# Ends of two expert stages: last down matrix in halves, output gates applied ahead of the 0/1 product, next first tile by column halves

## The chip, the cores and the metric

The kernel runs on one core of one Trainium2 chip. The metric is the device time of one execution in microseconds (us), the median of several runs. All data are 32-bit floats. A profiled execution comes with it, whose times below count from the start of its span. PE is the matrix engine (PEld its weight loads), DVE the vector engine, ACT the scalar engine, POOL the third elementwise engine; SP issues DMAs.

## What is computed

The program is a two-layer transformer block with mixture-of-experts layers, followed by a second, dense block of one layer. What matters here is the end of each expert layer, the residual sum, and the normalisation and projection that come next. D is 1024, a layer has 32 experts with an inner width of 512, and each token goes to two of them.

```python
f = _hier_moe(tokens, ...)        # per expert: (silu(x @ w_gate[e]) * (x @ w_up[e])) @ w_down[e]
                                  # out[token] += weight * result, for two experts per token
x = x + g2 * f[:b * s]            # g2: the output gates, one value per column
...
h = _modulate(_rmsnorm(x, norm1_g[i]), sh1, sc1)   # layer 1 starts: norm, then times (1+scale), plus shift
q, k, v = _project(h, w_qkv, splits)
...
return _rmsnorm(x, final_g)       # end of the first block
...
h = rms_norm(x, attn_norm_g) @ w_in                # second block starts
```

## The kernel before, in words

Each layer's expert stage is `experts` (L2200 to L2674). Tokens are grouped in blocks of 64 for one expert. For block i, PE multiplies the turned tokens by the gate matrix and the up matrix (`expand`, L2401), ACT and DVE form the hidden values, PE turns them (L2438), and `contract` multiplies them by the down matrix (L2447): 16 matmul records of 512 columns. The result `down` lies in PSUM with the two column halves of D on the two halves of the partitions, 64 tokens each. DVE copies it to `y` (L2632) and POOL scatters its rows into the DRAM tensor `y_dram` (`moe_results` in the trace). A ring of three slots holds each expert's three 2 MB matrices; SP issues the loads (`load_gate`, `load_up`, `load_down`) when a slot has been read, all in one queue.

Block 31, the last, is treated apart. Its rows are not waited for from DRAM. PE makes its `down`; ACT copies that to `ring["y"]` (L2521); PE multiplies a matrix of zeros and ones, `hit`, by that copy (`last_part`, L2127), which puts the rows of the head tile (the first tile of 128 tokens that the next stage takes up) in token order in the PSUM tiles `gate[0]` and `up[0]`, one for each half of the columns. DVE meanwhile adds up the other experts' share of that tile. The order on DVE is written out by hand, each instruction waiting for the one before:

- multiply the gates by the tile's weight of its last expert, `share` (L2663), once the gates are in;
- wait for `ys`, both result rows of each token of the head tile (`ys_in`), scale and add them (L2665, L2666), multiply by the gates (L2668), add to the residual `res` (L2669);
- wait for the 0/1 product (`part_done`), and for each column half multiply it by the scaled gates (L2673) and add it to `res` (L2674).

SP's order is: the gates broadcast to 128 partitions, 512 KB (L2299); wait until the scatters of the blocks before have landed; `ys`, 1 MB (L2302); then the next stage's first weights and vectors (`enter_1_loads`, `enter_2_loads`). The gates and `ys` lie in the ring's third down slot (`moe_wd` in the trace). A barrier of all engines ends the stage, and the next stage begins on the other side of it.

After layer 0 that is `enter_layer_1`: POOL scatters the last block's rows (L2135), SP then reads the results of the next tile and its gates (L2787, L2788). DVE norms the head tile (L2867, L2869), PE turns its eight column groups (L2923), ACT copies them to SBUF in two halves (L2811), and PE starts the projections (L2949), three chunks of eight matmuls. Before the third chunk PE turns the first chunk's rotated heads (L2932). For these it waits on DVE, whose order is norm of the head tile, sum of the next tile (`combine`, L2850 to L2853, behind its gates and results), rotation of the first chunk (L192 to L203).

After layer 1 it is `enter_block_2`: DVE applies both norms in one pass (L3244), PE turns (L3348), ACT copies (L3159), and PE does five chunks (L3362). In both stages PE runs some transposes of the identity (L1582) while it waits for the norm.

## Time and profile before

| what | value |
|---|---|
| median of 3 runs | 2636.52 us (2635.07 to 2636.66) |
| the profiled execution's own time | 2634.72 us |
| its span | 2632.8 us |
| PE busy | 2351.5 us (89%) |
| DVE busy | 1242.7 us (47%) |
| ACT busy | 571.0 us (22%) |
| layer 0's expert stage | about 590 to 1079 us of the span |
| layer 1's expert stage | about 1410 to 1888 us |

The times of the page are averages over stages with different limits. The part of the program that the change touches is short: some 20 us at the end of each expert stage and the beginning of the next. It is read from the timeline there, which lists instructions in order of time, with the idle time of the engine in brackets and what ended it.

### The profile page before, as it was taken

To read this page: it belongs to the slowest core of one execution; us is meant where nothing else is said; L and a number is where in the kernel's file an instruction comes from. 1 tells how busy PE (TensorE), PEld (TensorE's weight loads), DVE (VectorE), ACT (ScalarE), POOL (GpSimd) and SP (SyncE) were. 2 spreads that over 40 slices of the span, in tenths; PEclk is the share of its full clock that TensorE was granted. 3 is DMA by queue.
4 is the path that set the end of the run, shared out by engine and by line. 5 is a ranking of instruction groups with operands and counts; after the bars stand their busy time and mean duration, and the time that the engine had idled before them with its cause. 6 is when DMAs were issued, how large, how long until landed. Compare 5 with 4: busy or idle time off the path is not lost. (4 is left out here: it accounts for less than half of the span.)

```text
span 2632.8 us, 32518 instructions
## 1 busy us (share of the span) xinstructions
PE 2351.5 (89%) x12743; PEld 1383.2 (53%) x12743; DVE 1242.7 (47%) x2503; ACT 571.0 (22%) x1347; POOL 169.1 (6%) x268
## 2 busy tenths in 40 slices
PE   7999898988987777798998998788799899999999
PEld 4455666555543333445656553343344665888444
DVE  3367788754322222475655322222355653445665
ACT  4000487210100000115541100000122552111000
POOL 0000000002211111000001111111000000000000
PEclk9999999999999999999999999999999999999999
DMA  8774500449999999714019999999820221232643
GB/s 304 263 276 150 230 12 1 180 171 396 423 425 426 425 425 427 280 68 147 1 66 391 424 423 426 425 425 425 354 90 0 77 75 46 65 96 76 212 160 128
DMA packets 133380, 619.45 MB, mean 235 GB/s; under 512 B 21248, under 2 KB 48296, under 8 KB 103528
## 3 DMA queue, kind: packets, MB, share of 16 engines
q1 hardware_dynamic: 122664, 596.30, 57.1%
q0 software_dynamic: 10560, 21.01, 2.1%
q8 instruction: 105, 1.72, 0.3%
q14 instruction: 51, 0.42, 0.0%
HBM read 600.40 MB, written 30.47 MB: 240 GB/s over the span
## 5 line engine op out<-in xcount | busy, mean ns | idle before, releaser
L2401 PE MATMUL moe_gate<-moe_wg,moe_xg_t 128*64 128x256 f32 x1984 | 241.1, 394 | 49.1 <-DMA moe_wg<-in_moe_w_gate 47.5
L2401 PE MATMUL moe_up<-moe_wu,moe_xg_t 128*64 128x256 f32 x1984 | 239.2, 392 | 42.2 <-DMA moe_wu<-in_moe_w_up 42.2
L2447 PE MATMUL moe_down<-moe_wd,moe_hid_t 128*64 128x512 f32 x1024 | 235.5, 601 | 43.9 <-DMA moe_wd<-in_moe_w_down 30.8
L2401 PEld LDWEIGHTS moe_gate<-moe_wg,moe_xg_t 128*64 128x64 f32 x1984 | 147.5, 136 | 159.9 <-DMA moe_wg<-in_moe_w_gate 81.4
L2401 PEld LDWEIGHTS moe_up<-moe_wu,moe_xg_t 128*64 128x64 f32 x1984 | 146.1, 135 | 130.8 <-DMA moe_wu<-in_moe_w_up 60.6
L3847 PE MATMUL mlp_acc<-m_h,mlp_w 128*128 128x256 f32 x896 | 196.3, 382 | 5.3 <-DVE c_buffer L4024 2.5
L2632 DVE COPY moe_y<-moe_down 128x512 f32<-128x512 f32 x62 | 42.9, 692 | 308.1 <-PE moe_down L2447 308.1
L3847 PEld LDWEIGHTS mlp_acc<-m_h,mlp_w 128*128 128x128 f32 x896 | 171.0, 191 | 30.4 <-issue 4.1
L2447 PEld LDWEIGHTS moe_down<-moe_wd,moe_hid_t 128*64 128x64 f32 x1024 | 74.0, 137 | 161.2 <-issue 124.0
L2495 ACT ACTIVATE moe_sig<-moe_gate 128x256 f32<-128x256 f32 x64 | 24.5, 383 | 540.0 <-PE moe_gate L2401 540.0
L2619 DVE TENSOR_SCALAR moe_sig<-moe_sig 128x256 f32<-128x256 f32 x62 | 18.3, 294 | 257.3 <-ACT moe_sig L2495 257.3
L2621 DVE RECIPROCAL moe_sig<-moe_sig 128x256 f32<-128x256 f32 x62 | 108.7, 1753 | 2.1
L2336 POOL DMA_INDIRECT moe_results<-moe_y,moe_y_idx x62 | 64.2, 1035 | 705.3 <-DVE moe_y L2632 705.3
L2488 ACT COPY moe_xg_t<-moe_x_tp 128x512 f32<-128x512 f32 x64 | 37.4, 585 | 303.7 <-PE moe_x_tp L2385 303.7
L3898 PE MATMUL mlp_acc<-mlp_w,mlp_s_t 128*128 128x512 f32 x176 | 79.1, 592 | 0.0
L1117 ACT ACTIVATE dif_prob<-dif_score,dif_neg_max 128x768 f32<-128x768 f32 (+1 forms) x96 | 73.3, 764 | 13.9 <-DVE dif_neg_max L1049 9.7
L973 PE MATMUL dif_score<-a_k,a_q 64*128 64x256 f32 (+1 forms) x320 | 62.9, 504 | 14.8 <-ACT dif_prob L1117 12.5
L1333 DVE CUSTOM_DVE_ANT_0 swa_masked<-swa_score,b_masks,b_sinks 128x512 f32<-128x512 f32 (+1 forms) x64 | 52.1, 815 | 45.9 <-issue 32.3
L2627 DVE TENSOR_TENSOR moe_hid<-moe_sig,moe_up 128x256 f32<-128x256 f32 x62 | 26.1, 421 | 96.6 <-PE moe_up L2401 96.5
L2102 POOL DMA_INDIRECT moe_xg<-moe_tokens,moe_x_idx x62 | 64.6, 1042 | 49.0 <-POOL moe_x_idx L2312 48.2
L3898 PE MATMUL mlp_acc<-mlp_w,mlp_u_t 128*128 128x512 f32 x132 | 61.2, 592 | 0.0
L1006 PE MATMUL dif_out<-a_v,dif_prob_t 128*128 128x128 f32 x448 | 59.1, 278 | 2.2 <-ACTq L1134 0.9
(599 smaller groups left out, 3704.2 us busy)
## 6 DMA issues: line engine op xcount, KB each, us to landing
moe_wg<-in_moe_w_gate SPq DMA_DIRECT2D x64, 2048.0 KB, 41.9
moe_wu<-in_moe_w_up SPq DMA_DIRECT2D x64, 2048.0 KB, 42.8
moe_wd<-in_moe_w_down SPq DMA_DIRECT2D x64, 2048.0 KB, 42.4
qkv_mod_w<-in_mod_w SPq DMA_DIRECT2D x42, 1024.0 KB, 6.2
mlp_w<-in_w_down SPq DMA_DIRECT2D x44, 512.0 KB, 5.7
mlp_w<-in_w_up SPq DMA_DIRECT2D x16, 1024.0 KB, 8.0
qkv_w<-in_a_w_qkv SPq DMA_DIRECT2D x12, 1024.0 KB, 10.5
m_h<-in_w_down SPq DMA_DIRECT2D x20, 512.0 KB, 6.1
```

The source lines that it names most:

```text
L973: mm = nc.tensor.matmul(unit(g, m)[:, n0:n0 + w], q_t[rows, h, t * P:(t + 1) * P], k_t[rows, h, n0:n0 + w], start=True, stop=True)
L1006: mm = nc.tensor.matmul(out[:, 0:P], prob_t[:, g % 2, k, :], v[:, k, h * P:(h + 1) * P], start=(k == 0), stop=(k == keys(g) - 1))
L1117: nc.scalar.activation(prob[:, g % 3, m, 0:width], unit(g, m)[:, 0:width], ACT.Exp, bias=neg_max[:, g % 2, m:m + 1], accum_out=total[:, g ...
L1333: nc.vector.tensor_tensor_reduce(masked[:, g % 2, m, 0:width], score[m][:, 0:width], masks[:, b, 0:width], 1.0, sinks[:, 2 * c + m:2 * c + ...
L2102: nc.gpsimd.indirect_dma_start(ring["xg"][b][:], None, token_halves, bass.IndirectOffsetOnAxis(ap=places, axis=0), bounds_check=last_token ...
L2336: nc.gpsimd.indirect_dma_start(result_halves, bass.IndirectOffsetOnAxis(ap=y_idx[b][:], axis=0), y[b][:], None, bounds_check=last_result, ...
L2401: mm = nc.tensor.matmul(acc[b][halves[f], 0:HF], x_t[:, k, c, :], w[:, c, k, :].rearrange("p (q f j) -> p f q j", f=2, j=2)[:, f], start=( ...
L2447: mm = nc.tensor.matmul(down[b][halves[c], :], hid_t[:, k, h, :], wd[z][:, 2 * h + k, c * NCHUNK:(c + 1) * NCHUNK], start=(k, h) == (0, 0) ...
L2621: nc.vector.reciprocal(sig[:], sig[:]).then_inc(s["step"], 1)
L2632: nc.vector.tensor_copy(y[b][:], down[b][:]).then_inc(s["y_done"], 1)
L3847: mm = nc.tensor.matmul(acc[z][:, 0:half], lhs[:, k, j * P:(j + 1) * P], right_up(b)[:, k, :], start=(x < 4 and k == 0), stop=(k == 3), sk ...
L3898: mm = nc.tensor.matmul(bank(q, x)[:], lhs, rhs[:, f, :], start=(i == 0), stop=(i == 2 * MLP_GROUPS - 1), skip_group_check=True)
```

## The change

The last expert's down matrix comes in two DMAs, one for each half of the hidden values, each with a semaphore of its own; `contract` goes through the hidden values half by half (for all blocks, with the same matmuls), and for the last block waits for the second half in the middle. SP also loads the gates a second time as 64 rows by 512 columns for each column half, to the partitions where `down` holds that half. DVE no longer scales the gates by `share`. After it has added the other experts' share it multiplies `down` by those gates into `gated_y`; PE's 0/1 product reads `gated_y`; and DVE adds the product times `share` to `res`, one instruction for each column half. ACT's copy of `down` to `ring["y"]`, now only needed for the scatter, waits for `gated_y`. In the next stage, the head tile's norm is done by column halves, and PE's turns and first products wait for halves.

```diff
@@ load_down_in_halves, new
+    rows = e["moe_w_down"][layer].rearrange("x (p h k) n -> x p h (k n)", h=2, k=2)
+    for half, landed in enumerate((ring["d_in"][b], ring["tail_in"])):
+        part = ring["wd"][b][:, 2 * half:2 * half + 2, :]
+        sp.dma_start(part.rearrange("p a n -> p (a n)"), rows[x][:, half]).then_inc(landed, 16)
@@ experts, sync
+                if isinstance(x, int) and x == last:
+                    load_down_in_halves(sp, e, layer, ring, b, x)
+                else:
+                    load_down(sp, e, layer, ring, b, x)
...
             sp.dma_start(gates, bcast_rows(mod_part(e, layer, 5)(0))).then_inc(s["gates_in"], 16)
+            for half in range(2):
+                columns = mod_part(e, layer, 5)(0)[half * NCHUNK:(half + 1) * NCHUNK]
+                sp.dma_start(gates_by_half[HALVES[half], :], columns.partition_broadcast(HD)).then_inc(
+                    s["gates_in"], 16)
             sp.wait_ge(s["landed"], 2)
@@ contract
-                for k in range(2):
-                    for h in range(2):
+                for h in range(2):
+                    if h and by_halves:
+                        pe.wait_ge(ring["tail_in"], 16)
+                    for k in range(2):
@@ tensor, last block
-            pe.wait_ge(s["y_l_done"], 1)
-            last_part(nc, ring, part).then_inc(s["part_done"], 1)
+            pe.wait_ge(s["gated_done"], 1)
+            last_part(nc, ring, gated_y, part).then_inc(s["part_done"], 1)
@@ scalar, last block
-            act.wait_ge(s["downed"], i + 1)
+            act.wait_ge(s["gated_done"], 1)
             nc.scalar.copy(ring["y"][:], down[last % 2][:]).then_inc(s["y_l_done"], 1)
@@ vector, last block
-            link(v.tensor_scalar(gated_share, gates, ring["share"][:], None, ALU.mult))
...
             link(v.tensor_tensor(res, res, ys[:, 0, :], ALU.add))
+            dve.wait_ge(s["downed"], i + 1)
+            v.tensor_tensor(gated_y, down[b][:], gates_by_half, ALU.mult).then_inc(s["gated_done"], 1)
             dve.wait_ge(s["part_done"], 1)
             for half in range(2):
                 cols = slice(half * NCHUNK, (half + 1) * NCHUNK)
-                link(v.tensor_tensor(ys[:, 0, cols], part[half], gated_share[:, cols], ALU.mult))
-                link(v.tensor_tensor(res[:, cols], res[:, cols], ys[:, 0, cols], ALU.add))
+                link(v.scalar_tensor_tensor(res[:, cols], part[half], ring["share"][:], res[:, cols], ALU.mult,
+                                            ALU.add))
@@ enter_layer_1, vector (tile 0 by halves; enter_block_2 has the like in first_norms)
-                link(v.scalar_tensor_tensor(h[:], e["res"][:, t, :], rstd[:, one],
-                                            mul[:, side(t), :], ALU.mult, ALU.mult))
-                v.tensor_tensor(h[:], h[:], add[:, side(t), :], ALU.add).then_inc(s["h_done"], 1)
+                width = D if i else NCHUNK
+                for n0 in range(0, D, width):
+                    cols = slice(n0, n0 + width)
+                    link(v.scalar_tensor_tensor(h[:, cols], e["res"][:, t, cols], rstd[:, one],
+                                                mul[:, x, cols], ALU.mult, ALU.mult))
+                    v.tensor_tensor(h[:, cols], h[:, cols], add[:, x, cols], ALU.add).then_inc(s["h_done"], 1)
@@ both, tensor
-                pe.wait_ge(s["h_done"], i + 1)
                 for half in range(2):
+                    pe.wait_ge(s["h_done"], i + 2 if i else 1 + half)
...
+                    if j == 0 and k % 4 == 0:
+                        pe.wait_ge(s["n_tp_read"], 1 + k // 4)
```

On DVE, at the end of layer 0's expert stage (layer 1's reads the same), stood before, from the last hidden values on (`moe_wd` is the slot that holds the gates and `ys`, `moe_gate` and `moe_up` hold the 0/1 product's halves):

```order
L2659 TENSOR_TENSOR moe_hid<-moe_sig,moe_up 128x256
L2663 TENSOR_SCALAR moe_wd<-moe_wd,moe_last_share 128x1024
L2665 TENSOR_SCALAR moe_wd<-moe_wd,r_weight 128x1024
L2666 SCALAR_TENSOR_TENSOR moe_wd<-moe_wd,r_weight 128x1024
L2668 TENSOR_TENSOR moe_wd<-moe_wd 128x1024
L2669 TENSOR_TENSOR res<-res,moe_wd 128x1024
L2673 TENSOR_TENSOR moe_wd<-moe_gate,moe_wd 128x512
L2674 TENSOR_TENSOR res<-res,moe_wd 128x512
L2673 TENSOR_TENSOR moe_wd<-moe_up,moe_wd 128x512
L2674 TENSOR_TENSOR res<-res,moe_wd 128x512
```

The sums over the other experts' results (the rows from L2665 to L2669) stand between the scaled gates and the use of the product.

On DVE, at the same place, stands now (`moe_wd` on the left of `moe_down` is `gated_y`):

```order
L2678 TENSOR_TENSOR moe_hid<-moe_sig,moe_up 128x256
L2683 TENSOR_SCALAR moe_wd<-moe_wd,r_weight 128x1024
L2684 SCALAR_TENSOR_TENSOR moe_wd<-moe_wd,r_weight 128x1024
L2686 TENSOR_TENSOR moe_wd<-moe_wd 128x1024
L2687 TENSOR_TENSOR res<-res,moe_wd 128x1024
L2689 TENSOR_TENSOR moe_wd<-moe_down,moe_wd 128x512
L2693 SCALAR_TENSOR_TENSOR res<-moe_gate,moe_last_share,res 128x512
L2693 SCALAR_TENSOR_TENSOR res<-moe_up,moe_last_share,res 128x512
```

The pass over 1024 columns ahead of the sums is gone; behind them one pass of 512 from `down` is new, and the four of 512 behind the product have become two.

On SP, in the same stage, from the gates on, stood before:

```order
L2299 DMA moe_wd<-mod_scratch 128x1024
L2302 DMA moe_wd<-moe_results 128x2x1024
L2178 DMA moe_wu<-in_norm_g 128x1024
L2181 DMA moe_wg<-mod_scratch 128x1024
L2182 DMA moe_wg<-mod_scratch 128x1024
L2172 DMA moe_wg<-in_b_w_qkv 128x8x512
```

The second row is `ys`, the results of the head tile; the rows after it are the next stage's.

On SP, at the same place, stands now:

```order
L2312 DMA moe_wd<-mod_scratch 128x1024
L2315 DMA moe_wd<-mod_scratch 64x512 x2
L2319 DMA moe_wd<-moe_results 128x2x1024
L2187 DMA moe_wu<-in_norm_g 128x1024
L2190 DMA moe_wg<-mod_scratch 128x1024
L2191 DMA moe_wg<-mod_scratch 128x1024
L2181 DMA moe_wg<-in_b_w_qkv 128x8x512
```

Two broadcasts of 64 by 512 have come between the gates and `ys`.

On DVE, at the entry of layer 1, from the end of the head tile's inverse root on, stood before:

```order
L167 TENSOR_TENSOR qkv_rstd<-qkv_rstd,qkv_tmp 128x1
L2867 SCALAR_TENSOR_TENSOR qkv_h<-res,qkv_rstd,moe_wg 128x1024
L2869 TENSOR_TENSOR qkv_h<-qkv_h,moe_wg 128x1024
L2850 TENSOR_SCALAR qkv_ys<-qkv_ys,r_weight 128x1024
L2851 SCALAR_TENSOR_TENSOR qkv_ys<-qkv_ys,r_weight 128x1024
```

The norm of the tile is the second and third row; the sum of the next tile follows.

On DVE, at the same place, stands now:

```order
L167 TENSOR_TENSOR qkv_rstd<-qkv_rstd,qkv_tmp 128x1
L2890 SCALAR_TENSOR_TENSOR qkv_h<-res,qkv_rstd,moe_wg 128x512
L2892 TENSOR_TENSOR qkv_h<-qkv_h,moe_wg 128x512
L2890 SCALAR_TENSOR_TENSOR qkv_h<-res,qkv_rstd,moe_wg 128x512
L2892 TENSOR_TENSOR qkv_h<-qkv_h,moe_wg 128x512
L2870 TENSOR_SCALAR qkv_ys<-qkv_ys,r_weight 128x1024
L2871 SCALAR_TENSOR_TENSOR qkv_ys<-qkv_ys,r_weight 128x1024
```

The two passes over the tile have become four over its column halves.

## Rows read from the trace of the kernel before

**Rows 1.** Timeline, end of layer 0's expert stage: start us, us, engine, line, operation [idle before]

```profile
1055.34 0.33 SPq L2299 DMA_DIRECT2D moe_wd<-mod_scratch  x1
...
1066.09 0.37 SPq L2302 DMA_DIRECT2D moe_wd<-moe_results  x1
...
1070.86 0.58 ACT L2521 COPY moe_last_y<-moe_down 128x512 f32<-128x512 f32 x1 [3.93 <-PE moe_down L2447]
...
1071.59 0.66 PE L2127 MATMUL moe_gate<-moe_last_y,moe_last_hit 64*128 64x512 f32 x1 [0.77 <-ACT moe_last_y L2521]
...
1071.65 0.75 DVE L2665 TENSOR_SCALAR moe_wd<-moe_wd,r_weight 128x1024 f32<-128x1024 f32 x1 [2.82 <-DMA moe_wd<-moe_results]
...
1072.13 0.59 PE L2127 MATMUL moe_up<-moe_last_y,moe_last_hit 64*128 64x512 f32 x1
...
1075.02 1.22 DVE L2669 TENSOR_TENSOR res<-res,moe_wd 128x1024 f32<-128x1024 f32 x1
...
1076.28 0.69 DVE L2673 TENSOR_TENSOR moe_wd<-moe_gate,moe_wd 128x512 f32<-128x512 f32 x1
...
1078.45 0.69 DVE L2674 TENSOR_TENSOR res<-res,moe_wd 128x512 f32<-128x512 f32 x1
```

**Rows 2.** Timeline, end of layer 1's expert stage

```profile
1876.67 3.65 PE L2447 MATMUL moe_down<-moe_wd,moe_hid_t 128*64 128x512 f32 x16 [0.75 <-DMA moe_wd<-in_moe_w_down]
...
1880.74 0.75 DVE L2665 TENSOR_SCALAR moe_wd<-moe_wd,r_weight 128x1024 f32<-128x1024 f32 x1 [2.16 <-DMA moe_wd<-moe_results]
```

**Rows 3.** DMA issues (KB each, median us to landing): end of layer 0's stage

```profile
moe_wd<-moe_results SPq DMA_DIRECT2D x1, 1024.0 KB, 5.5
...
moe_wd<-mod_scratch SPq DMA_DIRECT2D x1, 512.0 KB, 12.7
```

**Rows 4.** DMA issues: end of layer 1's stage, then three loads into an idle queue

```profile
moe_wd<-moe_results SPq DMA_DIRECT2D x1, 1024.0 KB, 5.1
...
qkv_ys<-moe_results SPq DMA_DIRECT2D x3, 1024.0 KB, 5.2
```

**Rows 5.** Windows of 1 us: busy of the engines, granted clock, DMA share, GB/s

```profile
1077.00:1078.00 1.00, 0.00 (x0) 0.00 (x0) 0.96 (x2) 0.00 (x0) 0.00 (x0) 0.50 1.02 379
...
1886.00:1887.00 1.00, 0.00 (x0) 0.00 (x0) 0.93 (x3) 0.00 (x0) 0.00 (x0) 0.50 0.00 0
```

**Rows 6.** One line's instructions: duration ns min/median/max (the product of 512 columns)

```profile
L2949 PE MATMUL qkv_acc<-moe_wd,b_buffer x96: 592/592/1222, 1102.9 to 1201.6; 128*128 128x512 f32 x96
```

**Rows 7.** Timeline, entry of layer 1's projections

```profile
1080.68 1.13 POOL L2135 DMA_INDIRECT moe_results<-moe_last_y,moe_last_y_idx  x1 [22.61 <-issue]
...
1082.22 1.28 DVE L2867 SCALAR_TENSOR_TENSOR qkv_h<-res,qkv_rstd,moe_wg 128x1024 f32<-128x1024 f32 x1
...
1086.73 7.10 PE L2949 MATMUL qkv_acc<-moe_wg,b_buffer 128*128 128x512 f32 x16 [0.82 <-ACT b_buffer L2811]
...
1095.56 0.75 DVE L2850 TENSOR_SCALAR qkv_ys<-qkv_ys,r_weight 128x1024 f32<-128x1024 f32 x1 [10.79 <-DMA moe_wu<-mod_scratch]
...
1102.45 0.66 PE L2932 MATMUL qkv_tp<-ident_sb,qkv_stage 128*128 128x128 f32 x4 [1.75 <-DVE qkv_stage L203]
```

**Rows 8.** DMA over layer 1's entry (1072 to 1095 us): total, two issues

```profile
DMA packets 4469, 8.89 MB, mean 387 GB/s; under 512 B 1215, under 2 KB 1215, under 8 KB 4466
...
moe_wu<-in_b_w_qkv SPq DMA_DIRECT2D x1, 2048.0 KB, 10.9
...
qkv_rope<-const_axial SPq DMA_DIRECT2D x1, 256.0 KB, 11.6
```

**Rows 9.** Timeline, entry of the second block

```profile
1893.38 1.28 DVE L3244 SCALAR_TENSOR_TENSOR c_buffer<-c_buffer,in_n_rstd,res 128x1024 f32<-128x1024 f32 x1
...
1894.73 1.73 PE L3348 MATMUL in_tp<-ident_sb,c_buffer 128*128 128x128 f32 x8 [0.41 <-DVE c_buffer L3244]
...
1897.22 7.11 PE L3362 MATMUL in_acc<-moe_wg,in_h_tile 128*128 128x512 f32 x16 [0.77 <-ACT in_h_tile L3159]
```

**Rows 10.** Windows: the second block's projections from their first product

```profile
1897.00:2035.00 138.00, 135.60 (x350) 63.74 (x351) 69.41 (x174) 32.10 (x68) 0.00 (x0) 1.00 0.21 77
```

33 lines of the change are left out of this document (20 added, 13 removed).

## Prediction

> **What bounds the kernel now.** I read the page's first parts only to see that no single engine bounds the program, then the timeline at the ends of the two expert stages, where everything that is changed lies, then the DMA issues, the granted clock, and the entries of the two stages behind. For each wait on the way to the end of a stage the question is what came last.
>
> At the end of layer 0's expert stage there are two branches [rows 1]. PE's branch ends early: the 0/1 product starts at 1071.59 and is done at 1072.13 + 0.59 = 1072.72 us. DVE's branch is late: it waits for `ys` until 1071.65, sums until 1075.02 + 1.22 = 1076.24, and turns to the product at 1076.28, when that has lain ready for 3.6 us. The last addition ends at 1078.45 + 0.69 = 1079.14, and nothing else is at work. So the path is: landing of `ys`, four passes on DVE (4.6 us), and a tail of 1079.14 - 1076.24 = 2.90 us. The down matrix and the copy on ACT are not on it. Layer 1 reads alike: `ys` ends the wait at 1880.74, while the last down product began at 1876.67 and runs 3.65 us, to 1880.32 [rows 2].
>
> **The change, part by part.** *The down matrix in halves.* In layer 1 PE waited 0.75 us at most in front of the last down product [rows 2]; whatever of it goes, goes from the branch that is early by 3.6 us. I take 0. The second DMA issue costs SP some 0.4 us (the issues of rows 1 take 0.33 and 0.37) while it has nothing to do before 1066.09. The other order of hidden halves leaves every block's matmuls as they were: 0.
>
> *The gates once more.* Their 2 x 128 KB stand ahead of `ys` in SP's queue. At the 387 GB/s of a full queue [rows 8] 0.26 MB take 0.7 us. Is the queue still at work when `ys` comes? In layer 0 the gates were issued at 1055.34 and took 12.7 us, to 1068.04 [rows 1, 3], 2 us after `ys` was issued at 1066.09; `ys` took 5.5 us [rows 3], where the same megabyte takes 5.2 us in an idle queue [rows 4]. So it was held up a little, and I take 0.6 us. In layer 1 `ys` took 5.1 us [rows 4] and was not held up; most of the 0.7 falls into the gap, and I take 0.2. The bounds are 0 and 0.7 in each.
>
> By the ring order of one queue on each DMA engine (the Trainium skill, "DMA: Bandwidth & Descriptors", section "Queues, rings and completion order": descriptors are consumed in ring order) the two broadcasts would hold back `ys` by their whole 0.7 us in layer 1 too, and the sum below would be 0.5 us more; the 5.1 us beside 5.2 speaks for a queue that had run dry by then, and no run here shows the new broadcasts.
>
> *DVE's removed pass.* The scaled gates (1024 columns, 0.75 us like L2665) lay in the wait for `ys`: 0.
>
> *The tail.* This is the main term. Before: four passes, 2.90 us. Now, counted from the same 1076.24: `gated_y`, a two-operand pass from PSUM of 512 columns like L2673, 0.04 + 0.69; the hand-over to PE, as from ACT's copy (ends 1071.44) to the product (1071.59), 0.15; the product; the hand-over back, 0.06; two passes with a scalar of 512 columns. Their price is 0.75 each: over 1024 columns such a pass takes 1.28 [rows 7] and one without the scalar 1.22 [rows 1], so the scalar adds 0.06 to L2673's 0.69. With 0.04 between them they make 1.54. The product took 1.13 us at full clock [rows 1]. But PE has by then been idle since the last down product, in layer 0 from 1070.82 (ACT's copy follows at 1070.86) to about 1077.7, and the granted clock after the product of before had fallen to 0.50 by 1077 and by 1886 [rows 5], the lower level of 1.2 GHz, with PE idle since 1072.72 and about 1882. One 512-column matmul record runs 592 ns at full clock and up to 1222 when slowed [rows 6]; twice 1.13 is 2.3, less what is not the array's, and I take 2.2. The tail is 0.73 + 0.15 + 2.2 + 0.06 + 1.54 = 4.68 us, **1.78 longer** in each stage; at full clock it is 3.61, 0.71 longer. The product, which lay beside DVE's sums, now lies behind them.
>
> *ACT's copy and its table load* come behind `gated_y` and end some 2.1 us after it; DVE ends 3.95 after it (2.9 at full clock). Covered. The copy is read only after the barrier.
>
> *Layer 1's entry.* Halving the norm costs DVE two more fixed costs (four passes of about 0.7 to 0.75 for 1.28 and 1.22, some 0.45 us), but only four turns and no copy stand before PE's first product, which would come about 0.9 us earlier from the stage's start than 1086.73. That brings nothing to the end: PE stands still at 1102.45 for 1.75 us, for DVE's rotated heads, and DVE had waited until 1095.56 for the next tile's gates from DMA [rows 7]. With the stage 1.78 + 0.6 = 2.4 later and the first product 0.9 earlier, PE is 1.5 later, still inside the 1.75. So what counts here is when those gates land. They are issued once the scatter that POOL starts at 1080.68 has landed, which moves with the stage; but the queue is full over all of this stretch (387 GB/s; two loads issued as the stage starts, at about 1080, land only 10.9 and 11.6 us later [rows 8], the second near 1091.7), and the results and gates stand behind these: from 1091.7 to 1095.56 there is just time for their 1.5 MB at that rate. A start up to some 2.4 us later is, as I read it, still ahead of its turn. What does shift them is the added bytes: **+0.6 us** for layer 0's end. Bounds: 0, and 2.4 if the queue runs dry.
>
> *The second block's entry.* One pass of 1.28 becomes two of 0.75. PE's eight turns took 1.73 us at the lower clock, and the first product began 1897.22 - 1893.38 = 3.84 us after the norm's start [rows 9]. Now the first four turns can start at the end of the identity transposes, 1894.73 - 0.41 = 1894.32, eight are done at 1896.1, and the first copies lie beside the second four; the first product comes at about 1896.2: **-1.0 us** (bounds -0.5 and -1.4, by how far the clock has risen). Behind it PE is busy 135.6 of 138 us at full clock [rows 10], so this passes on whole. Layer 1's end: +1.78 + 0.2 - 1.0 = **+1.0 us**.
>
> **Sum.** 0.6 + 1.0 = +1.6 us. The profiled execution took 2634.72 us, so its like would take 2636.3; it lies 1.8 below the median of 2636.52, and the forecast for the median is 2638.1 us. A measurement of this kernel can tell about 0.2% (5.3 us) from no change; this is no change by that measure, on the slower side.
>
> **Rivals.** *Full clock at the product.* If the clock has not yet fallen when `gated_y` is ready, the tail is 0.71 longer: 0.5 in layer 0 and 0.71 + 0.2 - 1.0 = -0.1 in layer 1, together +0.4, 2636.9 us. Against it: rows 5, where the clock is down some 4 to 5 us after PE's last work, while the product now comes some 7 us after it. For it: the records show a fall in two places only.
>
> The Trainium skill ("TensorE: Matmul & The Clock Gate", "HAM oscillation — how this bites in real kernels") speaks against work put behind an idle stretch of PE, which then starts at the lower clock; rows 5 agree with their 0.50. The same page ("What's actually happening") says that the watch over PE's activity runs free of the kernel, so that the moment of a fall varies; by that the product of one stage could still find the full clock, and the sum would be 1.1 us less if it is layer 1's.
>
> *The delay passes whole into layer 1.* If the queue has run dry when the results of the next tile are issued, the 2.4 us of layer 0's end count instead of 0.6: +3.4, 2639.9 us. It decides where the last scatter's landing comes later than the load of 11.6 us. For it: my margin there is some tenths. Against it: the full rate [rows 8].
>
> *Results early.* If `ys` landed 3.6 us earlier, PE's branch would bound both kernels; the end would then need 0.69 + 0.15 + 1.13 + 0.06 + 1.54 after `down` instead of 1.9 + 2.90, 1.2 less, and layer 1's end would gain 1.2 + 1.0: 2634.3 us. Against it: both stages show the same wait [rows 1, 2].
>
> *Slow broadcasts: clearly slower.* If the rows of 64 move as slowly as the gates' 512 KB at worst (12.7 us [rows 3], so up to 6.4 us for 256 KB), `ys` is late by them and everything in layer 1's entry too. At 4 us it is 4 + 1.78 + 4 - 1.0 = +8.8, 2645.3 us; beyond 2.3 us it is over 0.2%. Against it: most of the gates' 12.7 us is the weights ahead of them.
>
> That the change does not do what its name says is within the forecast: the halves of the matrix end no wait that counts.
>
> **How the numbers follow.** Forecast 0.55, full clock 0.13, whole delay 0.17, results early 0.10, slow broadcasts 0.05. The range from 2635.2 to 2640.6 holds the first three with the spread of the runs (1.6 us) and the bounds above; the last two lie outside it but for a part of the fourth. Over 0.2% faster: no case gives it, 0.02 for the unforeseen. Slower: the slow broadcasts, 0.05. No change: 0.93.
>
> **What would show it.** `ys` waited for until about 0.6 us later in layer 0 and 0.2 in layer 1; the tail from the last sum to the last addition 4.7 us, with the product at a granted clock of 0.50 and about 2.2 us long; at layer 1's entry PE still waiting for the rotated heads, for less than 1.75 us; in the second block the first product 2.8 us after the norm's start instead of 3.84. The forecast is wrong if the tail is below 3.5 us, if `ys` comes more than 1 us later, or if PE no longer waits at layer 1's entry.

## The result and the profile after

The changed kernel takes 2649.05 us (median of 20 runs, 2637.62 to 2657.02) against 2637.99 for the kernel before (20 runs, 2634.79 to 2644.28): ratio 1.0038, 95% interval 1.0025 to 1.0051 (ratios, here and below, rest on all executions of both kernels and are not quotients of the medians). The forecast was 2638.1 with a range to 2640.6, so it was wrong: the change makes the kernel slower by more than the 0.2% that can be told.

The median hides the shape. Ten of the 20 executions lie between 2637.6 and 2643.9 (median 2641.2), ten between 2654.2 and 2657.0, and none between; the median itself lies in the empty stretch. Even the shorter ten lie above the forecast's range by their median. The kernel before has no such second group. Below, an execution is called *long* if it belongs to a group set off from the rest of its kernel by an empty stretch of 7 us or more. The profiled execution of the changed kernel is a long one (2655.46 us, span 2653.6, mean granted clock 0.968 against 0.981).

**Where the profiled execution loses.** Its anchors on TensorE, against those of before, shift by +1.5 us by the start of layer 0's expert stage (no part of the change lies ahead of it), by 2.3 us more over layer 0's end, by 2.2 us more over layer 1's end with the second block's entry, and then by 14.2 us inside the second block's attention.

The end of layer 0's expert stage, on the timeline (start us, us, engine, line, operation, out<-in; in brackets the idle time before and what ended it):

```profile
1056.44 0.33 SPq L2312 DMA_DIRECT2D moe_wd<-mod_scratch  x1
1056.44 0.69 DVE L2651 COPY moe_y<-moe_down 128x512 f32<-128x512 f32 x1 [4.80 <-PE moe_down L2466]
1056.81 1.77 SPq L2315 DMA_DIRECT2D moe_wd<-mod_scratch  x2
...
1066.04 0.38 SPq L2319 DMA_DIRECT2D moe_wd<-moe_results  x1
...
1073.78 0.75 DVE L2683 TENSOR_SCALAR moe_wd<-moe_wd,r_weight 128x1024 f32<-128x1024 f32 x1 [6.38 <-DMA moe_wd<-moe_results]
...
1078.40 0.69 DVE L2689 TENSOR_TENSOR moe_wd<-moe_down,moe_wd 128x512 f32<-128x512 f32 x1
...
1079.24 1.19 PE L2128 MATMUL moe_gate<-moe_wd,moe_last_hit 64*128 64x512 f32 x1 [6.98 <-DVE moe_wd L2689]
...
1081.36 0.75 DVE L2693 SCALAR_TENSOR_TENSOR res<-moe_gate,moe_last_share,res 128x512 f32<-128x512 f32 x1 [2.26 <-PE moe_up L2128]
1082.15 0.75 DVE L2693 SCALAR_TENSOR_TENSOR res<-moe_up,moe_last_share,res 128x512 f32<-128x512 f32 x1
```

These answer to [rows 1]. The result rows `ys` are asked for at 1066.04, as before, but waited for until 1073.78 instead of 1071.65. `gated_y` (L2689) follows the sums, the 0/1 product (L2128) starts at 1079.24, after 6.98 us of idle PE, with matmuls of 1.19 us where they took 0.66 at full clock, and its two adding steps (L2693) end at 1082.90. From the last sum (1077.15 + 1.22) to the last addition it is 4.53 us; the forecast was 4.68, before it was 2.90.

The DMA issues of that stretch (out<-in, queue, count, KB each, median us from issue to landing), beside [rows 3]:

```profile
moe_wd<-moe_results SPq DMA_DIRECT2D x1, 1024.0 KB, 7.6
...
moe_wd<-mod_scratch SPq DMA_DIRECT2D x2, 128.0 KB, 13.0
moe_results<-moe_y,moe_y_idx POOLq DMA_INDIRECT x1, 7.8
```

`ys` took 7.6 us instead of 5.5, and the two new gate broadcasts 13.0 us (their median). The scatter that `ys` waits for landed in 7.8 us; before it took 9.0.

Layer 1's end reads alike (timeline), beside [rows 2]:

```profile
1868.34 0.69 DVE L2651 COPY moe_y<-moe_down 128x512 f32<-128x512 f32 x1 [4.76 <-PE moe_down L2466]
...
1885.56 0.75 DVE L2683 TENSOR_SCALAR moe_wd<-moe_wd,r_weight 128x1024 f32<-128x1024 f32 x1 [6.26 <-DMA moe_wd<-moe_results]
...
1891.02 1.19 PE L2128 MATMUL moe_gate<-moe_wd,moe_last_hit 64*128 64x512 f32 x1 [6.87 <-DVE moe_wd L2689]
...
1893.92 0.75 DVE L2693 SCALAR_TENSOR_TENSOR res<-moe_up,moe_last_share,res 128x512 f32<-128x512 f32 x1
```

To have a measure free of the shift, I count from DVE's copy of the block before the last (L2632 before, L2651 now), whose scatter has to land ahead of `ys`. Before, the copy of layer 0 starts at

```profile
1055.34 0.69 DVE L2632 COPY moe_y<-moe_down 128x512 f32<-128x512 f32 x1 [4.81 <-PE moe_down L2447]
```

so the sums start 16.31 us after it (1071.65) and the stage ends 23.80 us after it (1079.14); in layer 1 it is 16.36 and 23.86. Now it is 17.34 and 26.46 in layer 0, 17.22 and 26.33 in layer 1. **Each stage ends 2.5 to 2.7 us later**: about 0.9 to 1.0 in the wait for `ys`, 1.6 in the tail.

Layer 1's entry (timeline, SP, DVE and PE) and, under it, two windows (stretch, busy time of PE, PEld, DVE, ACT, POOL with instruction counts, granted clock, DMA share, GB/s), beside [rows 7, 8]:

```profile
1083.79 0.38 SPq L2181 DMA_DIRECT2D moe_wu<-in_b_w_qkv  x1
...
1099.35 0.75 DVE L2870 TENSOR_SCALAR qkv_ys<-qkv_ys,r_weight 128x1024 f32<-128x1024 f32 x1 [10.10 <-DMA moe_wu<-mod_scratch]
...
1106.23 0.66 PE L2955 MATMUL qkv_tp<-ident_sb,qkv_stage 128*128 128x128 f32 x4 [2.20 <-DVE qkv_stage L203]
```

```profile
1082.00:1085.00 3.00, 1.16 (x6) 1.19 (x7) 1.99 (x4) 1.03 (x2) 0.16 (x1) 0.50 0.77 276
1085.00:1088.00 3.00, 3.00 (x16) 3.00 (x15) 2.54 (x9) 0.41 (x3) 0.98 (x1) 0.50 0.92 300
```

The next tile's gates land at 1099.35, 3.79 us later than before, as the stage's end is 3.76 later (1082.90 against 1079.14). PE waits for the rotated heads 2.20 us, where it waited 1.75; the forecast had it wait less. The DMA queue moved 276 and 300 GB/s as the stage began, not 387: it was not full. Before, at the same place in the stage, it was full (its first load, on the timeline, and the first window from it):

```profile
1079.63 0.38 SPq L2172 DMA_DIRECT2D moe_wu<-in_b_w_qkv  x1
```

```profile
1079.00:1082.00 3.00, 2.32 (x11) 2.35 (x12) 2.06 (x7) 1.45 (x3) 1.13 (x1) 0.50 1.04 398
```

The second block's entry (timeline, DVE and PE), beside [rows 9]:

```profile
1899.81 1.42 DVE L3271 SCALAR_TENSOR_TENSOR c_buffer<-c_buffer,in_n_rstd,res 128x512 f32<-128x512 f32 x2
...
1902.50 7.93 PE L3392 MATMUL in_acc<-moe_wg,in_h_tile 128*128 128x512 f32 x16
1910.26 7.03 PE L3392 MATMUL in_acc<-moe_wu,in_h_tile 128*128 128x512 f32 x16
```

The first product starts 2.69 us after the norm's start (2.8 forecast, 3.84 before). But it runs 7.93 us instead of 7.11, because the granted clock is 0.50 until 1904.2.

The start of the second block's attention, in windows, first before, then after, the latter about 6 us later:

```profile
2072.00:2076.00 4.00, 2.22 (x16) 1.54 (x15) 2.82 (x12) 1.53 (x2) 0.00 (x0) 1.00 0.37 102
2076.00:2080.00 4.00, 2.58 (x16) 1.79 (x14) 2.22 (x12) 3.99 (x15) 0.00 (x0) 1.00 0.84 290
...
2082.00:2106.00 24.00, 24.00 (x177) 19.07 (x177) 12.69 (x54) 18.05 (x57) 0.00 (x0) 1.00 0.01 1
```

```profile
2078.00:2082.00 4.00, 2.22 (x16) 1.51 (x15) 2.83 (x12) 1.46 (x2) 0.00 (x0) 0.96 0.31 100
2082.00:2086.00 4.00, 3.90 (x12) 2.81 (x11) 1.74 (x10) 3.95 (x14) 0.00 (x0) 0.50 0.84 291
2086.00:2115.00 29.00, 29.00 (x114) 22.03 (x113) 8.49 (x40) 11.73 (x36) 0.00 (x0) 0.50 0.00 1
2115.00:2119.00 4.00, 4.00 (x27) 3.42 (x26) 1.86 (x8) 2.32 (x7) 0.00 (x0) 0.90 0.00 0
```

In the first four microseconds the two do the same work: PE is busy 2.22 us of 4. Before, the clock stays at 1.00. After, it falls at 2081.7 to 0.50, the lower level of 1.2 GHz, and stays there until 2115.8, although the records show PE busy for the whole of 29 us. That is the 14 us: the attention ends 20.3 us later than before, having begun 6.1 later.

### The profile page after: what moved, and what is told of

It is laid out like the page before. It is cut to its first block and busy times, and to the rows that moved or that the text cites. A ratio compares the mean times of both kernels' runs of the same rounds, so it can differ in the third digit from the quotient of the medians.

```text
span 2653.6 us, 32532 instructions
## 1 busy us (share of the span) xinstructions
PE 2375.3 (90%) x12743; PEld 1400.2 (53%) x12743; DVE 1240.3 (47%) x2502; ACT 571.8 (22%) x1347; POOL 169.1 (6%) x268
## 5 line engine op out<-in xcount | busy, mean ns | idle before, releaser
L2651 DVE COPY moe_y<-moe_down 128x512 f32<-128x512 f32 x62 | 42.9, 691 | 308.4 <-PE moe_down L2466 308.4
## 6 DMA issues: line engine op xcount, KB each, us to landing
qkv_w<-in_a_w_qkv SPq DMA_DIRECT2D x12, 1024.0 KB, 10.6
```

The lines of the kernel that those rows point to most:

```text
L2651: nc.vector.tensor_copy(y[b][:], down[b][:]).then_inc(s["y_done"], 1)
```

## Experiments

Two questions: what makes the long executions, and what the ends of the stages cost apart. Each kernel was timed beside runs of the kernel before on the same chip. Beside the experiments the kernel before has 124 executions, and 20 beside the changed kernel: none of the 144 is long, the slowest takes 2647.85 us (one more, of 6084 us, is left out).

The experiments ran on three chips: the first four on one; the entry by halves alone, the change without it, the down matrix in halves and the three edits together on a second; the others on a third. On the second chip no execution of any kernel was long, so a missing long group says little there.

**A pure delay on the kernel before.**

```diff
                 link(v.tensor_tensor(res[:, cols], res[:, cols], ys[:, 0, cols], ALU.add))
+            if layer == 1:
+                for _ in range(4):
+                    link(v.tensor_tensor(ys[:, 1, :], ys[:, 1, :], gates, ALU.mult))
```

> The kernel before with nothing changed but four dead products of 1.26 us each on VectorE at the end of layer 1's expert stage, 5.0 us in all. Theory A (arrival): the 14 us that the changed kernel lost in the second block's attention hang on the moment at which that attention begins, not on what the change does; then a share of the executions here stands at about 2638 + 5 = 2643 us and a share at about 2643 + 14 = 2657 us, and a profile of the longer kind has a granted clock of 0.50 for over 30 us there. Theory B (content): the operations that the change adds bring the clock down; then all executions lie between 2640 and 2646 us. Theory C (chance): the kernel before has the long kind as well and was lucky in its 20 runs; then it shows in the runs of the kernel before that go with this one.

2644.54 us (2640.57 to 2647.23, 11 runs), ratio 1.0025 [1.0016, 1.0033], no long execution. The attention began at 2081.7, later than in the changed kernel, and kept its clock (windows):

```profile
2080.00:2084.00 4.00, 2.22 (x16) 1.57 (x15) 2.82 (x12) 1.42 (x2) 0.00 (x0) 1.00 0.31 98
...
2088.00:2117.00 29.00, 27.86 (x204) 22.16 (x204) 14.83 (x65) 22.40 (x72) 0.00 (x0) 1.00 0.01 2
```

A late arrival alone does not do it: theory A falls, and so does chance.

**More work for TensorE at the attention's start.**

```diff
+            spare = out[1][:].rearrange("p a d -> p (a d)")
             scores(0)
             scores(1)
+            busy_array(nc, e, spare, 5)
             for g in range(n + 1):
                 if g + 2 < n:
                     scores(g + 2)
+                if g < 3:
+                    busy_array(nc, e, spare, (8, 4, 4)[g])
```

> The changed kernel with 25 more identity transposes on TensorE, in the first 10 us of the second block's attention, where it waits for the exponentials. If the clock falls there because TensorE works too little (theories A and B alike), no execution is over 2646 us and the median is about 2641 us, the level of the changed kernel's shorter executions, with at most 1 us for the transposes. Rival: the fall has nothing to do with TensorE's work at this place; then executions at 2654 to 2657 us stay, and the median remains near 2649.

2642.01 us (2640.27 to 2643.33, 11 runs), ratio 1.0011 [1.0002, 1.0020], no long execution. The edit adds 21 transposes (the expectations say 25). In the windows PE is busy 2.92 of the first 4 us instead of 2.22, and the clock stays:

```profile
2078.00:2082.00 4.00, 2.92 (x20) 2.08 (x19) 2.83 (x12) 1.65 (x2) 0.00 (x0) 1.00 0.37 110
2082.00:2086.00 4.00, 3.89 (x28) 3.15 (x27) 2.09 (x12) 3.99 (x15) 0.00 (x0) 1.00 0.77 284
2086.00:2115.00 29.00, 27.91 (x206) 22.21 (x206) 14.85 (x65) 21.97 (x72) 0.00 (x0) 1.00 0.01 2
```

On the same chip two kernels with the second block's entry of the change and without the transposes had 11 long executions of 24 (the next two experiments). So the 14 us hang on TensorE's thin work there, and some 0.8 us (2642.0 against 2641.2) is the price of the transposes. That these help by shifting the instructions behind them, and not as work, no run excludes.

**Without the gate broadcasts.**

```diff
-            for half in range(2):
-                columns = mod_part(e, layer, 5)(0)[half * NCHUNK:(half + 1) * NCHUNK]
-                sp.dma_start(gates_by_half[HALVES[half], :], columns.partition_broadcast(HD)).then_inc(
-                    s["gates_in"], 16)
...
-            v.tensor_tensor(gated_y, down[b][:], gates_by_half, ALU.mult).then_inc(s["gated_done"], 1)
+            for half in range(2):
+                cols = slice(half * NCHUNK, (half + 1) * NCHUNK)
+                v.tensor_tensor(gated_y[HALVES[half], :], down[b][HALVES[half], :], gates[HALVES[half], cols],
+                                ALU.mult).then_inc(s["gated_done"], 1)
```

> The changed kernel without the two gate broadcasts by halves: the last block's rows are multiplied by the gates that are there already, in two products of 64 rows. Theory: the broadcasts ahead of the results on the queue are what made these take 7.6 and 7.8 us from issue to landing; without them 5.1 to 5.5 us, so the stages end 2.1 - 0.7 = 1.4 us earlier in layer 0 and 2.7 - 0.7 = 2.0 us earlier in layer 1 (0.7 is the second product), 2637.8 us where the attention keeps its clock and 14 more where not. Rival: the results were slow for the load on memory by the next weights, not for the broadcasts; then 7.6 us stays and both stages end 0.7 us later.

2639.06 us (2636.62 to 2655.15, 12 runs), ratio 1.0018 [1.0001, 1.0035]; 5 of the 12 are long, the other seven have a median of 2638.7, 2.5 under the changed kernel's shorter ones. Timeline of layer 0's end, and the landing of `ys`:

```profile
1055.90 0.69 DVE L2647 COPY moe_y<-moe_down 128x512 f32<-128x512 f32 x1 [4.80 <-PE moe_down L2462]
...
1064.49 0.37 SPq L2315 DMA_DIRECT2D moe_wd<-moe_results  x1
...
1071.42 0.75 DVE L2679 TENSOR_SCALAR moe_wd<-moe_wd,r_weight 128x1024 f32<-128x1024 f32 x1 [5.00 <-DMA moe_wd<-moe_results]
...
1076.04 1.41 DVE L2687 TENSOR_TENSOR moe_wd<-moe_down,moe_wd 64x512 f32<-64x512 f32 x2
...
1080.50 0.75 DVE L2692 SCALAR_TENSOR_TENSOR res<-moe_up,moe_last_share,res 128x512 f32<-128x512 f32 x1
```

```profile
moe_wd<-moe_results SPq DMA_DIRECT2D x1, 1024.0 KB, 6.8
```

The sums start 15.52 and 15.43 us behind the copy (layer 0, layer 1) instead of 17.34 and 17.22: **the broadcasts cost 1.8 us in each stage** of this pair; over the four profiles with them `ys` lands 7.2 to 7.9 us after its issue, over the twelve without them 5.1 to 6.8. Here `ys` itself took 6.8 us and not 5.5, yet came earlier, since it was asked for earlier: the stage then gains even against before (16.3). That part is the down matrix in halves, below.

**The gated rows ahead of the sums.**

```diff
+            dve.wait_ge(s["downed"], i + 1)
+            v.tensor_tensor(gated_y, down[b][:], gates_by_half, ALU.mult).then_inc(s["gated_done"], 1)
             dve.wait_ge(s["ys_in"], 16)
...
-            dve.wait_ge(s["downed"], i + 1)
-            v.tensor_tensor(gated_y, down[b][:], gates_by_half, ALU.mult).then_inc(s["gated_done"], 1)
             dve.wait_ge(s["part_done"], 1)
```

> The changed kernel with the gated rows of the last block computed as soon as the block's sums are there, before the results are waited for, so that the 0/1 product (2.1 us) and the gating (0.7 us) lie beside the four sums of the results. Theory: the tail behind the sums shrinks from 4.5 us to the two adding steps of 0.77 us, 3.0 us a stage; passed on whole in both layers that is 6 us, about 2635 us where the attention keeps its clock. Rival 1: layer 0's part is absorbed at layer 1's entry by its gates, which are waited for as before; then about 2638 us. Rival 2: the halves of the gates land later than the results, so that the sums start later; then the gain is under 1 us a stage.

2642.21 us (2635.27 to 2655.41, 12 runs), ratio 1.0017 [0.9998, 1.0036]; 6 of 12 are long, the other six have a median of 2637.0, 4.1 under the changed kernel's shorter ones. The timeline shows the product beside the sums, at full clock (0.66 us a matmul), and only the two adding steps behind them:

```profile
1074.29 0.69 DVE L2683 TENSOR_TENSOR moe_wd<-moe_down,moe_wd 128x512 f32<-128x512 f32 x1 [4.97 <-PE moe_down L2466]
1074.90 0.74 DVE L2685 TENSOR_SCALAR moe_wd<-moe_wd,r_weight 128x1024 f32<-128x1024 f32 x1
...
1075.13 0.66 PE L2128 MATMUL moe_gate<-moe_wd,moe_last_hit 64*128 64x512 f32 x1 [0.95 <-DVE moe_wd L2683]
...
1080.31 0.75 DVE L2693 SCALAR_TENSOR_TENSOR res<-moe_up,moe_last_share,res 128x512 f32<-128x512 f32 x1
```

The stages end 24.16 and 24.20 us behind the copy: 2.2 us earlier than in the changed kernel. Less than 3.0, because the sums wait for `gated_y`.

**The second block's entry by halves alone, and the change without it.**

```diff
-                v.scalar_tensor_tensor(h, h, n_rstd[:, 1, 0:1], g, ALU.mult, ALU.mult).then_inc(s["h_done"], 1)
+                for half in range(2):
+                    cols = slice(half * NCHUNK, (half + 1) * NCHUNK)
+                    v.scalar_tensor_tensor(h[:, cols], h[:, cols], n_rstd[:, 1, 0:1], g[:, cols], ALU.mult,
+                                           ALU.mult).then_inc(s["h_done"], 1)
...
-                pe.wait_ge(s["h_done"], i + 1)
                 for half in range(2):
+                    pe.wait_ge(s["h_done"], i + 2 if i else 1 + half)
...
-                if c == 0:
+                if c == 0 and i:
...
+                    if j == 0 and k % 4 == 0:
+                        pe.wait_ge(s["tp_read"], 1 + k // 4)
```

> The kernel before with one part of the change alone: at the second block's entry the first tile is normed and turned by column halves. Theory D (entry): whether the granted clock falls at the start of the second block's attention is set by how TensorE's first product of the block stands to the rise of the clock, and this part moves that product up by 1.1 us and takes the idle time between turn and product away; then a third to a half of the executions stands about 14 us over the rest, and the rest at 2637 us, 0.3 to 1.0 under the kernel before. Rival (another part of the change does it): no execution over 2646 us.

2636.57 us (2634.01 to 2645.57, 11 runs), ratio 0.9999 [0.9990, 1.0009], no long execution. By itself that spoke against theory D; but it ran on the chip on which nothing was long. The changed kernel with the diff above taken back:

> The changed kernel with the second block's entry as it was before; all the rest of the change stays. Theory D: no execution is over 2648 us, and the median is that of the changed kernel's shorter executions and up to 1 us more, 2641.2 to 2642.2 us, since the stages' ends cost about 2.5 us each as before. Rival: a third to a half of the executions still stands near 2655 us.

2642.65 us (2641.39 to 2645.74, 11 runs), ratio 1.0019 [1.0010, 1.0028], no long execution, as theory D has it, on the same chip, so that this proves little. I took both results at their word: they left only an interaction (entry by halves *and* a later arrival) or the changed tail's own work, so I put the first to the test: the entry by halves with nothing of the tail, and a delay (the dead products of the first experiment, two or four).

> The kernel before with the second block's entry by column halves and two dead products of 1.26 us on VectorE at the end of layer 1's expert stage. Theory E (two conditions): the 14 us in the second block's attention want both the entry by halves, which brings the attention's start from 10.2 to 10.9 us behind the last rise of the granted clock down to 8.2 to 9.0 us, and a later arrival; then some executions, two or more of 11, stand near 2652 us and the rest near 2636.6 + 2.5 = 2639. Rival F (the tail's content): later arrival alone does nothing, the changed tail's own work on TensorE is wanted; then no execution is over 2648 us.

> As the run before with four dead products, 5.0 us. Theory E: some executions, two or more of 11, near 2655 us and the rest near 2641.6; rival F: none over 2650 us.

Two products: 2642.93 us (2635.64 to 2657.00, 12 runs), ratio 1.0024 [1.0009, 1.0040], 4 of 12 long (2651.2 to 2657.0). Four: 2643.64 us (2638.68 to 2656.68, 12 runs), ratio 1.0032 [1.0017, 1.0047], 4 of 12 long (2652.4 to 2656.7). The tail's work is not needed; rival F falls. Against the pure delay without the entry by halves (0 of 11) and the kernel before on the chip of these two runs (0 of 57), it is the entry by halves that these two have more.

**The down matrix in halves alone.**

```diff
-                load_down(sp, e, layer, ring, b, x)
+                if isinstance(x, int) and x == last:
+                    load_down_in_halves(sp, e, layer, ring, b, x)
+                else:
+                    load_down(sp, e, layer, ring, b, x)
...
-                for k in range(2):
-                    for h in range(2):
+                for h in range(2):
+                    if h and by_halves:
+                        pe.wait_ge(ring["tail_in"], 16)
+                    for k in range(2):
```

> The kernel before with one part of the change alone: the last down matrix in two halves, its product over halves in turn. Theory: with the halves the scatter of the block before the last lands in 7 to 8 us after its issue instead of 9.0 and 9.4, so the results are asked for earlier and the sums start 15.5 us behind that block's copy instead of 16.3; both stages end 0.8 us earlier, 2636 to 2636.5 us. Rival (the forecast's): the halves do nothing, 2637 to 2638.5 us and sums 16.3 us behind the copy.

2636.22 us (2633.13 to 2639.13, 11 runs), ratio 0.9994 [0.9985, 1.0003]. The total can't tell, the timeline and the DMA issues can:

```profile
1056.30 0.69 DVE L2646 COPY moe_y<-moe_down 128x512 f32<-128x512 f32 x1 [4.80 <-PE moe_down L2461]
...
1071.71 0.75 DVE L2679 TENSOR_SCALAR moe_wd<-moe_wd,r_weight 128x1024 f32<-128x1024 f32 x1 [1.82 <-DMA moe_wd<-moe_results]
```

```profile
moe_wd<-moe_results SPq DMA_DIRECT2D x1, 1024.0 KB, 6.3
...
moe_results<-moe_y,moe_y_idx POOLq DMA_INDIRECT x1, 7.3
```

The sums start 15.41 and 15.22 us behind the copy. Over all profiles with the matrix whole (six) it is 15.96 to 16.63, over those with halves and no broadcasts (five) 15.18 to 15.52: no overlap, **some 0.9 us gained in each stage** (by means 0.8 in layer 0 and 1.0 in layer 1). The scatter lands in 7.3 us (7.5 in layer 1) instead of 9.0 (9.4); over all profiles it is 6.8 to 7.9 with halves and 8.8 to 9.5 without.

**Three edits together:** no broadcasts, the gated rows ahead of the sums, and the transposes.

```diff
+            dve.wait_ge(s["downed"], i + 1)
+            for half in range(2):
+                cols = slice(half * NCHUNK, (half + 1) * NCHUNK)
+                v.tensor_tensor(gated_y[HALVES[half], :], down[b][HALVES[half], :], gates[HALVES[half], cols],
+                                ALU.mult).then_inc(s["gated_done"], 1)
             dve.wait_ge(s["ys_in"], 16)
```

> The changed kernel with three edits together: no gate broadcasts by halves (two products of 64 rows on the gates that are there), these products ahead of the results' sums, and the 25 identity transposes at the start of the second block's attention. If the parts add up, a stage's end lies 22.0 to 22.7 us behind the copy of the block before the last, against 23.8 in the kernel before and 26.4 in the changed one, no execution shows the 14 us, and the median is 2634 to 2636.5 us, 0.05 to 0.15 per cent under the kernel before. Rival: the two 64-row products push the four sums back and the results, early or not, are waited for as long; then a stage's end is at 23.5 or later and the median at 2637 to 2639.

2637.57 us (2633.42 to 2639.39, 11 runs), ratio 0.9997 [0.9988, 1.0007], no long execution (on the chip where nothing was long): as fast as before, not faster. The rival came true, by a cause I had not named (DVE's timeline):

```profile
1074.73 1.41 DVE L2681 TENSOR_TENSOR moe_wd<-moe_down,moe_wd 64x512 f32<-64x512 f32 x2 [4.97 <-PE moe_down L2462]
1076.18 0.75 DVE L2684 TENSOR_SCALAR moe_wd<-moe_wd,r_weight 128x1024 f32<-128x1024 f32 x1
```

DVE now waits for the last block's down product until 1074.73, and the sums, whose `ys` took 5.6 us, stand behind it. The stages end 26.44 and 25.37 us behind the copy. The parts do not add up, because one queue of instructions waits for two late things in a fixed order.

**A tail without gated rows.** The product joins the weighted results *before* the gates are multiplied: (results + share x product) x gates. That takes the 0/1 product as it was before.

```diff
-            link(v.tensor_tensor(ys[:, 0, :], ys[:, 0, :], gates, ALU.mult))
-            link(v.tensor_tensor(res, res, ys[:, 0, :], ALU.add))
             dve.wait_ge(s["part_done"], 1)
             for half in range(2):
                 cols = slice(half * NCHUNK, (half + 1) * NCHUNK)
-                link(v.tensor_tensor(ys[:, 0, cols], part[half], gated_share[:, cols], ALU.mult))
-                link(v.tensor_tensor(res[:, cols], res[:, cols], ys[:, 0, cols], ALU.add))
+                link(v.scalar_tensor_tensor(ys[:, 0, cols], part[half], ring["share"][:], ys[:, 0, cols],
+                                            ALU.mult, ALU.add))
+            link(v.tensor_tensor(ys[:, 0, :], ys[:, 0, :], gates, ALU.mult))
+            link(v.tensor_tensor(res, res, ys[:, 0, :], ALU.add))
```

> The kernel before with the last down matrix in halves, and a tail that needs no gated rows: the 0/1 product of the last block's rows joins the two weighted results before the gates, so that the four closing steps of 0.69 us and the share's step become two adding steps of 0.75 us ahead of the gate product. Theory: 1.3 us less behind the results in each stage, passed on whole as in the runs so far, and 0.8 us each for the halves: 2637.1 - 2.6 - 1.6 = 2633 us, if the 0/1 product is there 2 us behind the start of the sums. Rival: the product comes later than that (a down product that starts 13 us or more behind the copy of the block before it) and is waited for, which eats the gain; then 2636 us, as with the halves alone.

2636.40 us (2634.42 to 2642.49, 12 runs), ratio 0.9997 [0.9988, 1.0005]: no better than the halves alone (2636.22). That is the rival's number, but not by its wait: DVE waited for the product 0.57 us in layer 1 and not at all in layer 0. The stages do end 21.58 and 21.88 us behind the copy, 2.2 and 2.0 earlier than before, but what is gained does not arrive: in layer 0 the third chunk starts 24.98 us after the stage's end instead of 23.80, in layer 1 the second block's first chunk ran 9.19 us, largely at the lower clock, instead of 7.11. The second may be chance: over the five profiles with the entry as before that chunk took 7.11, 7.11, 8.83, 9.19 and 9.34 us.

With the second block's entry by halves added (the diff of that experiment):

> As the run before, with the second block's entry by column halves as well. Theory: 0.3 to 0.7 us less than that, 2632.5 us, no execution with the 14 us, since the arrival is no later than in the kernel before (theory E). Rival: the entry by halves alone is enough in some executions; then one or more near 2647 us.

2636.94 us (2633.03 to 2649.58, 12 runs), ratio 1.0004 [0.9991, 1.0016]; two executions, 2649.12 and 2649.58, are long, **without any delay**: the rival, not theory E. The other ten have a median of 2636.4. In this profile the product was late in layer 1, and DVE waited for it:

```profile
1884.84 0.75 DVE L2684 SCALAR_TENSOR_TENSOR moe_wd<-moe_gate,moe_last_share,moe_wd 128x512 f32<-128x512 f32 x1 [1.99 <-PE moe_up L2128]
```

**The last two, with the transposes.** First this kernel, then the entry by halves with four dead products.

```diff
+                if g < 3:
+                    busy_array(nc, e, spare, (8, 4, 4)[g])
```

> The kernel before with the last down matrix in halves, the regrouped tail, the second block's entry by column halves and the 25 identity transposes at the start of that block's attention. Theory (thin work at the attention's start): no execution is 12 us or more over the rest, and the median is that of the shorter executions without the transposes, 2636.0, or up to 0.8 us more, against some 2638 for the kernel before in the same job. Rival: long executions near 2649 us stay (two of 12 or so).

2635.29 us (2633.03 to 2636.63, 11 runs), ratio 0.9989 [0.9980, 0.9997], no long execution: **faster than both kernels**, by 0.1% against before; the interval leaves 1 out, if narrowly, and it is one of fourteen kernels that were tried. The first and the last pass of its tail (DVE, layer 0):

```profile
1072.41 0.75 DVE L2678 TENSOR_SCALAR moe_wd<-moe_wd,r_weight 128x1024 f32<-128x1024 f32 x1 [4.94 <-DMA moe_wd<-moe_results]
...
1077.35 1.22 DVE L2687 TENSOR_TENSOR res<-res,moe_wd 128x1024 f32<-128x1024 f32 x1
```

> The kernel before with the second block's entry by column halves, four dead products (5.0 us) at the end of layer 1's expert stage and the 25 identity transposes. Theory: none of the executions near 2655 us is left (4 of 12 without the transposes), and the median is that of the shorter ones, 2642 to 2643.5 us. Rival: a third of the executions stays near 2655 us.

2641.92 us (2638.78 to 2648.94, 12 runs), ratio 1.0013 [1.0004, 1.0023]. Eleven lie within 2638.8 to 2644.0; the twelfth, at 2648.94, is 5.0 over the next and stands by itself, short of the 2652 to 2657 that were long without the transposes (4 of 12). It isn't long by the rule above, but its mean granted clock is 0.969, where the eleven have 0.974 to 0.979: it lost clock somewhere, and no profile of it shows where.

**The count of long executions.** Second block's entry by halves, without the transposes: 10 of 20, 5 of 12, 6 of 12, 0 of 11, 4 of 12, 4 of 12, 2 of 12 (changed kernel, no broadcasts, gated rows first, entry alone, two and four dead products, regrouped), 31 of 91. Entry by halves with the transposes: 0 of 45. Entry as before: 0 of 45, besides the kernel before's 144. Without the second chip it is 31 of 80, 0 of 34 (one of them the doubtful 2648.94) and 0 of 23. In the kernels with a long group the long executions have a mean granted clock of 0.967 to 0.974, the shorter ones 0.972 to 0.979; where the clock was lost is seen in the profiles of three long executions (changed kernel, no broadcasts, gated rows first), each time within 5 us of the attention's start, for 31 to 34 us. Shown, then: the entry by halves brings the long executions, and the start of the attention, where TensorE's work is thin, is the place where it happens. A later arrival is not needed; whether it makes them more frequent (8 of 24 with a pure delay against 2 of 12 with the regrouped tail, on the same chip) stays open. So does what the second chip does otherwise.

## Why the prediction was wrong

**The step that failed first: that behind the second block's entry everything passes on unchanged.** The forecast took -1.0 us for the entry and let it "pass on whole", on a PE busy 135.6 of 138 us at clock 1.00 [rows 10]. That stretch ends at 2035. The attention behind it begins with PE busy 2.22 us of 4, and there the clock can fall, in a third of the executions with the entry by halves and in half of those of the changed kernel, by the count above. The cost of one lasting fall, 14 us, is nine times the whole sum of the forecast. No rival held it. The shorter executions, too, are 3.2 us over the kernel before and not 1.6; that is the work of the steps that follow.

How a product that starts 1.1 us earlier can decide this, the profiles suggest but do not prove. With the entry as before, the attention starts 10.2 to 10.9 us after the clock's last rise (before, pure delay, change without the entry, halves alone, regrouped tail); with the entry by halves and no transposes it starts 8.2 to 10.0 us after it (seven profiles), and the profiles with a fall have 8.2, 8.2, 9.0 and 9.4 (the last one short, 3.4 us). Before, PE idled 0.77 us between the turns and the first product [rows 9]; the change without this part shows it still (PE's timeline), and the change has no idle time there:

```profile
1899.86 1.44 PE L3373 MATMUL in_tp<-ident_sb,c_buffer 128*128 128x128 f32 x8 [0.41 <-DVE c_buffer L3269]
1902.12 7.11 PE L3387 MATMUL in_acc<-moe_wg,in_h_tile 128*128 128x512 f32 x16 [0.82 <-ACT in_h_tile L3184]
```

The Trainium skill ("TensorE: Matmul & The Clock Gate", "What's actually happening") says that the watch over PE's activity runs free of the kernel, so that the same kernel can get different clocks from run to run. The mean granted clock of the changed kernel's executions agrees: 0.967 to 0.970 in the ten long ones, 0.973 to 0.977 in the others.

**Layer 1's entry: +0.6 forecast of 2.4, most of the delay measured.** The step was that a full DMA queue absorbs a late stage. It failed because the loads that fill the queue are issued as the stage begins, and so move with it (the first at 1083.79, before at 1079.63): 276 to 300 GB/s at the start instead of 398. The gates came 3.79 us later for a stage 3.76 later. That was the second rival, which I gave 0.17; its +3.4 us, 2639.9, is near the shorter executions' 2641.2 and their +3.2 over the kernel before. From the end of the stage to the third chunk it takes 23.80 us before, 23.82 in the changed kernel. Two more profiles with the same late end have 23.08 and 23.47, and the six with stage and entry as before lie between 23.47 and 24.21, so up to 0.9 us may be won there, by absorption or by the entry's halves; the profile of the change is at one end. The absorption is clearer on the other side: where the stage ended earlier than before (the regrouped tails), it takes 24.8 to 25.3.

**The gates once more: +0.6 and +0.2 forecast, 1.8 in each measured** (without the broadcasts against with). I priced them by bytes, 0.26 MB at 387 GB/s; two loads of 64 rows of 2 KB took 13.0 us to land ahead of `ys`. The bounds (0 and 0.7) did not hold it; the rival with slow broadcasts had the mechanism at 4 us.

**The down matrix in halves: 0 forecast, -0.9 in each stage measured.** I looked for its effect at PE, where there is none. It lies in DMA: the scatter ahead of `ys` lands some 1.5 to 2 us earlier. Why a weight load in two pieces does that, no run here tells. Together the last two give +0.9 to 1.0 in the wait for `ys` (1.03 in layer 0, where more than 1 was named as a sign of being wrong). That this is near the forecast's 0.6 in layer 0 is luck, two errors of opposite sign.

**The tail: +1.78 forecast, +1.63 measured** (4.53 against 2.90). Right, by its own steps: PE idle for 6.98 us, the product at the lower clock, 2.08 us for 2.2. The experiment with the gated rows first takes it away.

**The second block's entry: -1.0 forecast.** The start of the first product moved by 1.15 us as worked out, but it then ran at the lower clock until 1904.2 and 0.3 us were left in this pair of profiles. The pair understates it: of the five profiles with the entry as before, three ran that product partly at the lower clock (8.83 to 9.34 us), the one of the kernel before did not (7.11). From the norm's start to the second chunk it is 9.6 to 10.6 us in the eleven profiles with the entry by halves and 10.5 to 13.3 in the five without. By medians the entry was worth 0.7 us on the kernel before (2636.57 against 2637.26), 1.4 on the change (2642.65 against 2641.2, not timed side by side) and nothing on the regrouped tail (2636.4 both, without the long ones); the first is within the noise, and the others have no interval. So the term itself isn't refuted; what failed is that it passes on.

In sum the stages' ends cost some 5 us, of which 3.2 are left in the shorter executions (what the two entries gave back of it, no run splits exactly), and half of the executions paid 14 more.

## What to carry to other kernels

An edit that moves TensorE's work by a microsecond can have a second price where the engine's work is thin later on: look in the trace for such places behind the edit, run enough executions to see a second group, and put cheap work there if one shows. Before counting a delay as absorbed by a busy queue, ask when the transfers that fill it are issued; if they wait for the same stage, they move with it. Price a small broadcast by the landing of one like it, not by its bytes, and before putting new work in front of a late product see whether the sum can be regrouped so that the old product still fits.
